# Nine copies of modulation rows move from ScalarE to VectorE in the first attention

## The reference

```python
proj = rmsnorm(h, norm1_g) @ w_in                 # 1024 x 5120: q, k, v of 8 + 8 heads, and two gates
# heads 0-7: softmax(q k / 8 - slope * distance) v, causal (256 tokens are one block)
# heads 8-15, stick breaking, strictly causal:
z = (q @ k.T) * scale
log_1m = where(strict, log_sigmoid(-z), 0.0)
suffix = cumsum(log_1m, reverse=True) - log_1m
w = where(strict, exp(log_sigmoid(z) + suffix), 0.0)
# second block, layers i = 0 and 1, vectors c (latent tokens) and c_ctx (context tokens):
sh1, sc1, g1, sh2, sc2, g2 = split(silu(c) @ mod_w[i] + mod_b[i], 6)
a = rms_norm(h, norm_mix_g[i]) * (1.0 + sc1) + sh1
```

## Time and profile before

| | us |
|---|---|
| median of 3 runs | 1922.74 |
| lowest, highest | 1917.42, 1927.09 |
| the profiled execution's time | 1926.99 |
| its span | 1924.9 |
| TensorE busy in it | 1728.8 (90%) |
| VectorE busy | 1191.4 (62%) |
| ScalarE busy | 606.5 (32%) |

### The profile page before, as it was taken

How to read it: one execution, slowest core, us unless ns; L and a number is a source line. 1 busy time by engine, 2 the same in 40 slices (tenths; PEclk the granted TensorE clock), 3 DMA queues, 4 the chain that set the end, 5 groups by cost and what they waited for, 6 DMA issues and landing times.

```text
span 1924.9 us, 25418 instructions
## 1 busy us (share of the span) xinstructions
PE 1728.8 (90%) x10050; PEld 1344.0 (70%) x10050; DVE 1191.4 (62%) x2095; ACT 606.5 (32%) x919; POOL 572.8 (30%) x570
## 2 busy tenths in 40 slices
PE   7999999698879789898869888999999988989999
PEld 6776688565626356666536656989999644569999
DVE  4344363777797686678787577655553279735553
ACT  4346534211121122221211114334533223635442
POOL 0111100377666656666766660000000100000000
PEclk9998999899999989998979999999999999999999
DMA  8998875699999989999999994526554213025653
GB/s 278 322 322 289 294 252 170 242 397 409 409 384 410 409 330 409 409 409 408 408 409 409 409 402 148 193 91 197 177 194 134 80 50 102 1 88 180 191 181 125
DMA packets 223421, 515.93 MB, mean 268 GB/s; under 512 B 13325, under 2 KB 122205, under 8 KB 223325
## 3 DMA queue, kind: packets, MB, share of 16 engines
q0 software_dynamic: 86784, 318.80, 42.8%
q1 hardware_dynamic: 136192, 195.71, 29.9%
q10 hardware_dynamic: 348, 0.11, 0.0%
HBM read 513.53 MB, written 1.05 MB: 267 GB/s over the span
## 4 chain that ended last, share of the span: by engine, by line
PE 58%; DMA 17%; DVE 10%; POOL 6%; issue 4%; ACT 3%; another core or an unknown queue 1%; SPq 0%; ACTq 0%; DVEq 0%; POOLq 0%
PE bank L874 10%; DMA more<-in_peer_v_dram,idx 10%; PE bank L877 10%; PE bank L875 10%; POOL more L773 6%; PE bank L1192 6%; PE wide L1240 5%; DMA more<-in_peer_u_dram,idx 3%; PE bank L828 2%; PE wide L989 2%; DVE more L2288 2%; DVE rstd L2363 2%; DMA weights<-in_w_in_dram 2%; PE wide L1462 1%
## 5 line engine op out<-in xcount | busy, mean ns | idle before, releaser
L1904 DVE TENSOR_TENSOR low_weights<-weights,high_weights 128x2048 fp32r<-128x2048 f32 x108 | 247.4, 2292 | 308.4 <-ACT high_weights L1561 307.9
L2288 DVE CUSTOM_DVE_ANT_0 more<-more,wide 128x1024 f32<-128x1024 f32 x256 | 310.8, 1218 | 143.7 <-DMA more<-in_peer_u_dram,idx 113.7
L874 PE MATMUL bank<-high_input,high_weights 128*128 128x256 f32 x1312 | 375.5, 286 | 17.0 <-DVE low_input L1953 8.2
L875 PE MATMUL bank<-high_input,low_weights 128*128 128x256 f32 x1344 | 379.9, 283 | 0.0
L877 PE MATMUL bank<-low_input,high_weights 128*128 128x256 f32 x1312 | 372.6, 284 | 0.0
L1240 PE MATMUL wide<-more,rstd 128*128 128x512 f32 x476 | 243.9, 648 | 114.6 <-ACT rstd L1744 84.4
L773 POOL DMA_INDIRECT more<-in_peer_u_dram,idx x256 | 274.2, 1071 | 166.3 <-DVE dots L2288 70.3
L1561 ACT ACTIVATE high_weights<-weights 128x2048 fp32r<-128x2048 f32 x108 | 206.6, 1915 | 317.0 <-DMA weights<-in_ffn_w_gate_dram 91.4
L773 POOL DMA_INDIRECT more<-in_peer_v_dram,idx x256 | 253.0, 988 | 137.5 <-issue 67.5
L874 PEld LDWEIGHTS bank<-high_input,high_weights 128*128 128x128 f32 x1312 | 250.6, 191 | 28.6 <-issue 24.9
L1192 PE MATMUL bank<-nrm,weights 128*128 128x256 f32 x1088 | 249.2, 388 | 13.2 <-DVE big L1904 6.5
(11 more groups left out here) (267 smaller groups left out, 2328.2 us busy)
## 6 DMA issues: line engine op xcount, KB each, us to landing
weights<-in_ffn_w_down_dram SPq DMA_DIRECT2D x33, 1024.0 KB
weights<-in_ffn_w_gate_dram SPq DMA_DIRECT2D x30, 1024.0 KB
weights<-in_ffn_w_up_dram SPq DMA_DIRECT2D x30, 1024.0 KB
weights<-in_conv_w_in_dram SPq DMA_DIRECT2D x24, 1024.0 KB
weights<-in_w_in_dram SPq DMA_DIRECT2D x20, 1024.0 KB
nrm<-in_mod_w_dram POOLq DMA_DIRECT2D x14, 1024.0 KB, 8.0
sq<-in_mod_w_dram POOLq DMA_DIRECT2D x13, 1024.0 KB, 6.7
h_ctx<-in_mod_w_dram POOLq DMA_DIRECT2D x13, 1024.0 KB, 7.2
```

Of the source, the lines that this page charges most:

```text
L874: first = nc.tensor.matmul(out, cut(high), hi, start=start, stop=False, **more_args)
L875: nc.tensor.matmul(out, cut(w_lo[b]), hi, start=False, stop=False, **more_args)
L1904: return nc.vector.tensor_tensor(out, a, b, op)
L2288: nc.vector.tensor_tensor_reduce(u, u, wide[0][:, :], 1.0, 0.0, ALU.mult, ALU.add, dots[:, n % 16:n % 16 + 1]).then_inc(s_dot, 1)
```

## The change

ScalarE no longer copies the modulation rows for the nine quads that end in the loop of steps (chunks 7 to 39); it keeps the one after chunk 3 and the two after chunks 43 and 47. VectorE gets a `mod_rows` of its own with the same waits and the same semaphore, called after `front(s)` and `back(s-1)` and ahead of `low`. VectorE's loop gets two more steps, 17 and 18, in which only such a copy can stand. ScalarE's copies of the turned rows to `mod` stay where they were.

```diff
--- before.py
+++ after.py
@@ -1599,7 +1599,7 @@
             def mod_rows(j):
 
                 quad = j // MOD_PARTS
-                if j % MOD_PARTS == MOD_PARTS - 1:
+                if j % MOD_PARTS == MOD_PARTS - 1 and not FIRST - 1 <= j < LATE_MODS[0]:
                     act.wait_ge(s_mod_used, j + 1)
                     if quad >= 2:
                         wait_full(act, "mod_turn", quad - 2)
@@ -2099,13 +2099,26 @@
                     settle(last)
                     tt(logit[:, c], logit[:, c], expo[:, c], ALU.subtract).then_inc(s_arg, 1)
 
-            for s in range(HALVES + 1):
+            def mod_rows(j):
+
+                quad = j // MOD_PARTS
+                if j % MOD_PARTS == MOD_PARTS - 1:
+                    v.wait_ge(s_mod_used, j + 1)
+                    if quad >= 2:
+                        wait_full(v, "mod_turn", quad - 2)
+                    nc.vector.tensor_copy(mrow[:, quad % 2, :], sbank[3]).then_inc(s_mod_left, 1)
+
+            for s in range(HALVES + 3):
                 if s < HALVES:
                     front(s)
-                if s >= 1:
+                if 1 <= s <= HALVES:
                     back(s - 1)
+                for j in beat_mods(s)[:1]:
+                    mod_rows(j)
                 if s in BEAT and BEAT[s] + 3 < 20:
                     low("qkv", BEAT[s] + 3)
+                for j in beat_mods(s)[1:]:
+                    mod_rows(j)
 
 
             def low_mixed(g):
```

## The result

| | before | after |
|---|---|---|
| median, first comparison | 1923.45 us (4 runs) | 1945.15 us (4 runs) |
| ratio, 95% interval | | 1.0118 [1.0091, 1.0146] |
| median, second comparison | 1912.72 us (23 runs) | 1934.41 us (6 runs) |
| ratio, 95% interval | | 1.0116 [1.0085, 1.0147] |
| profiled execution and its span, first comparison | 1926.99, 1924.9 | 1937.7, 1935.9 |

Forecast was 1940 us against a median of 1922.74, a loss of 17.6 us; measured are 21.7 us in both comparisons. The two traced executions of the first comparison are only 10.7 us apart: that of the kernel before was among its slowest, that of the changed kernel the fastest of its four.

The account below looks back on a forecast made before the run. TensorE was taken to set the pace in the first attention; overruns of VectorE's copies plus one slow clock spell summed to 17.6 us, giving 1944.6 from the profiled execution or 1940.3 from the median, stated as 1940; range 1929 to 1949.

Parts of the forecast that it names:

- TensorE sets the pace and a hole is paid in full: First attention: TensorE has a stretch without holes, so whatever makes it wait is paid in full.
- The two kinds of terms: First attention: holes where TensorE waits for VectorE's copy, plus one new half-clock spell of 5.17 us; together 17.6 us.
- The copy: One copy of a quad of modulation rows on VectorE: taken as 0.68 us, bounds 0.55 and 0.75.
- Step 1: Copy after modulation chunk 7: TensorE loses 2.94 us, then one new slow clock spell costs 5.17.
- Step 3: Next copy after step 1: overrun 2.28 us, less 1.34 for the slower chunk and 0.4 for easing, leaves 0.5.
- Steps 5 and 7: Two copies of one pattern: 1.12 us lost each, eased by 0.4 each, 1.4 together.
- Step 9: No projection chunk behind the copy: 5.60 us more on top of the existing 1.91; the existing spell only starts later.
- Steps 11 and 13: Step 11's overrun is covered up to 0.91 us by TensorE's existing wait; step 13 loses 0.40.
- Step 15: No chunk in between: overrun 2.23 us, 0.68 covered by a transfer wait, 1.55 lost.
- Nothing is given back later: Behind the first attention: the rest of the kernel moves as a block, its span as long as before.
- The rival with two new spells: Slow clock spells at steps 1 and 15, another 5.2 us: 22.8 us lost, 1945; chance 0.16.
- The rival by which ScalarE had been the late one: VectorE reaches step 9's copy first, the 1.91 us hole and its spell go: about 8 us faster, 1915; chance 0.04.

Follow-up runs that it names:

- the five traces: Changed kernel with no further edit, traced once in the first comparison and four more times; its second-comparison median was 1934.41 us, ratio 1.0116.
- the two fastest versions: Kernel before with ScalarE's `high` of weight chunk 17 behind step 9's copy: with `low` also moved behind `front` and `back` 1907.30 us, alone 1907.87.
- only step 1: Against the kernel before, VectorE copies the modulation rows only in step 1, ScalarE makes the other copies: 1918.92 us, ratio 1.0039.
- the complement: Against the kernel before, VectorE copies in the seven steps other than 9 and 15, ScalarE in those two: 1921.88 us, ratio 1.0054.
- `low` moved alone: Kernel before with only VectorE's `low` moved behind the next step's `front` and `back`, all copies on ScalarE: 1911.31 us, ratio 1.0000.

## Why the prediction was right, step by step

- *TensorE sets the pace and a hole is paid in full.* TensorE is busy for 89 to 98% of the stage in every trace, and its own work in it is constant. But holes can stand in for each other: the 0.91 us of step 13 and the 0.68 in front of the transfer in step 15 are gone where an earlier hole has grown, as the sum assumed.
- *The two kinds of terms.* The holes of the forecast add up to 12.4 us; the five traces have 11.5 to 15.1 more than before, 12.7 in the mean. The clock term of the forecast is 5.2 us; the five traces have from 1.7 less to 7.5 more than before, 3.5 more in the mean. So the holes were forecast well; that the total came out near the forecast is in part luck, since the clock's share changes from one execution to the next.
- *The copy.* 0.68 us taken; nine rows of 0.683 to 0.691.
- *Step 1.* 2.94 forecast for the hole, 2.36 waited; the spell 5.17 forecast, 4.66 in the first trace (85.58 to 99.83 is 14.25 us, against 9.59 in the earlier trace rows). It came in three of five traces.
- *Step 3.* 0.5 forecast: none in the first trace, where the spell had slowed the chunk ahead; 1.75 in the second, where there was no spell. The other three agree: none behind a spell, 1.69 without one. The trade between the two that the sum assumed is there.
- *Steps 5 and 7.* 1.4 together; 1.21 + 0.22, and 0.87 + 0.21 in the second trace. The easing taken for shorter transfers is about right, though nothing isolates it.
- *Step 9.* This is the mis-sized term. The hole is right (7.5 forecast, 7.60). The forecast said that the spell there only starts later and costs the same. In the first trace only 3 us of work were done in it, instead of 10: from the end of the hole to modulation chunk 26 it is 11.55 us (172.56 to 184.11) against 14.76 in the earlier trace rows. 5.6 forecast, 5.7 - 3.2 = 2.5 measured. In the second trace it was 3 us of work again; in the other three the spell held 11 to 13 us, as before or worse. In all five it began inside the hole, where it costs nothing; what differs is when it ended. Below are the spell of the second trace and that of the third, whose holes end at 170.07 and 171.17:

```profile
166.70:173.50 6.80, 3.43 (x14) 1.48 (x15) 3.15 (x6) 4.71 (x6) 0.71 (x1) 0.50 0.06 26
165.80:182.80 17.00, 11.63 (x48) 7.36 (x49) 8.27 (x14) 8.69 (x12) 1.43 (x2) 0.50 0.55 182
```

  Why it ended sooner in two of five stays open.
- *Steps 11 and 13.* 0.4 forecast, 0.5 measured: 1.45 lost in step 11 (against about 1.1 assumed), 1.0 given back at the slack of step 13, as argued.
- *Step 15.* 1.55 without a spell; 2.9 measured, for a short spell of 3 us followed. In the other four traces it was 3, 7, 3 us and none.
- *Nothing is given back later.* The part behind the stage is 1679 to 1683 us in the twelve traces of the later comparisons, whatever the version; the kernel before isn't among them, and in the first comparison's pair it is 1696.8 before and 1692.2 after.

The sum came to 17.6; the five traces have 11.8 to 19.1 over the 171.0 of before, 16.1 in the mean. The rival with two new spells (22.8) names the right places in three of the five, which have spells at steps 1, 9 and 15; but these three lost 14.6, 18.6 and 19.1 us, nearer to the forecast, since the spell at step 15 was short. The rule of the Trainium skill that was set against the rows in the prediction ("TensorE: Matmul & The Clock Gate", "What's actually happening": half rate is the default, activity releases it) pointed to that case; the traces agree on the places in three of five. The rival by which ScalarE had been the late one fell; half of it, that ScalarE's copy of step 9 was late for its own reason, turned out true and is what the two fastest versions use.

What stays open: the median loses 21.7 us, the traced executions 16 in the stage. Two things on record would close most of this, and neither is shown. The kernel before was traced once, with 10 us of work in its spell at step 9; three other traces in which ScalarE makes that copy behind the same `high` (only step 1, the complement, `low` moved alone) have 0, 0 and 3 us there. If that is as common in the kernel before, its stage is on average about 168 us and not 171, and the loss in it about 19 (estimates from these four traces and the five of the changed kernel). And the traced executions of the changed kernel were quick ones: the untraced ones of the second comparison have a mean clock of 0.951 to 0.954 when they take 1933 us and more, and 0.960 at 1921.9; a third or fourth long spell would fit, but no trace caught such an execution.

## What to carry to other kernels

What the move cost was decided here by what stood ahead of the copy in each engine's queue, not by the engine's load. So before moving an instruction compare, copy by copy, when each queue reaches it with when the consumer asks. An instruction that waits for a transfer shouldn't stand ahead of one that the pacing engine waits for, if its own consumer is steps away; moving it behind cost nothing measurable here (1.0000 [0.9987, 1.0014] in the kernel before) and took back 18 of 22 us in the changed one. Look for such an order on the engine that has the work now before giving the work to another.

## What the runs showed of the hardware

In the stages of all 14 traces a slow spell followed no single hole up to 1.75 us. It followed nine of eleven holes between 1.90 and 2.71 us (not the 2.25 and 2.61 of step 1 in two traces of the changed kernel), seven of eight of 3.04 us, and all seven over 3.1. Once it followed two short holes, of 0.91 and 1.28 us, 2 us apart. Behind the same hole of 7.6 to 8.7 us at step 9 the work done at half rate was 3, 3, 12, 11 and 13 us in five executions of the changed kernel. Half rate is priced by the work that falls into it, not by its own length: the part of a spell that lies inside a hole costs nothing. Over the whole stage half of the slow time differs by up to 9 us between these five (half of 6.8 against half of 25.3), the holes by 3.5, and the length by 7.3. So one trace of such a kernel is uncertain by some 7 us.
